# A two-layer hybrid trunk: the first layer's opening rebuilt, the filter network moved to the last scan

## The chip, the cores and the metric

One core of one Trainium2 chip runs the whole program. The metric is the device time of one execution in microseconds; each time of a kernel is the median of several executions. The profile is of one further execution. TensorE (PE) has two clock levels, 1.2 and 2.4 GHz; the profile gives the granted clock as a share of the upper one.

## The reference

Two layers work on 640 tokens of width 1024: 512 latent tokens and 128 context tokens, each group with its own conditioning vector. Per layer:

```python
shift, scale, gate = split(silu(cond) @ w_mod + b_mod, 3)      # cond (1024), w_mod (1024, 3072)
h = rmsnorm(x, g_pre) * (1 + scale) + shift
proj = h @ w_in                       # 8208 columns: four mixers of 2048, and 16 for A's decay and beta
ya = gated_delta_rule(conv3(q, k, v), decay, beta) * silu(z)   # A, 4 heads, scan over chunks, two directions
yb = hyena(...)   # B, long filters from a small network: sin(sin(feat @ w1 + b1) @ w2 + b2) @ w3 + b3
yc, yd = neighbourhood_attention(...), differential_attention(...)
y = sum_k sigmoid(h @ w_merge_k + b_k) * (y_k @ w_branch_k) @ w_out
x = x + gate * rmsnorm(y, g_post)
```

Everything is float32 outside and inside. Large products are made of three: weights and activations are split into a high part and a rest (`hi`, `lo`), and hi·hi, hi·lo and lo·hi are added.

## The kernel before

The engines run programs of their own, in an order written out by hand; they meet in semaphores, each wrapped in a `Signal` with a starting value. The functions named below follow in the listing.

**Start.** SP raises 120 semaphores to their starting values (L366), then `started`, for which every engine waits (L355) before its first load or its first work. SP then loads x, six pairs of modulation blocks, the first block of `w_in`, two more pairs, and the further weight blocks. POOL's queue loads nine constants (L447, all engines wait for all nine), then the filter network's weights and features, `lam`, the gate columns and the level masks (L458 to L468).

**Modulation, first layer.** w_mod's blocks for the 1024 shift and the 1024 scale channels go in pairs: pair p is the p-th block of 128 shift channels and the p-th of 128 scale channels. `mod_products` (PE) multiplies the conditioning (two columns padded to 32) with both blocks, 32 matmuls, into rows spread over four groups of 32 partitions. `rows_out` (ACT) copies them to `mod_rows`. `mod_channels` (PE) turns rows to channels and adds the four groups by a matmul with `pick`, a 128 x 2 matrix of ones at the right places. DVE adds the bias and makes `g_scale`. The rows of w_mod come through four slots: `raw` 0-1, `raw` 2-3 and two in `merged`. Further sixteen pairs (post gate and layer 1) go one by one into the merges (`later_pair`, L328), three in each merge as long as there are any.

**Activations, first layer.** ACT sums the squares of five tiles (L1466), POOL takes the power -1/2 (L456), DVE scales (L2035). PE turns x by transposes, eight times five (`turn_input`), after pair 1; ACT copies each turned k to `xT`; with pair p's channels ACT makes `modulated(p-1)`, and DVE splits it (`h_split`). When all eight pairs are through, PE runs the eight pieces of the first block (`project(..., KT)`, 6 matmuls a piece), then the 16 gate columns in both halves (`ab_half`), then block 1 with small turns of the gates between its pieces.

**The filter network.** Per layer two products of 64 rows by 640 (`hidden`), each followed by an argument reduced to one turn on DVE (`argument`, six operations) and a sine on ACT. Layer 0 does it at the very start; layer 1's stands in layer 0's output stage. B is the first to use its result, late in A's merge.

**Head 0.** Behind the gate columns come softplus, exp and sums (DVE L2060 to L2080, ACT L1487 to L1495). PE waits for their last result, `ab_done`, then runs block 2. ACT splits blocks 2 and 3 (`split_hi`) and then takes block 0 from PSUM; DVE does its share (`split_lo`), then the convolutions. `A_front` turns the convolved tiles, and so on; 16 fronts a head. Then levels of the triangular solve and five scan steps (`A_scan`, `A_step`); with the last head, PE fills the scan's gaps with pieces of the merge's first block (`last_part`). After the scan DVE squares the outputs, POOL takes the power, DVE norms them, PE turns them for the merge.

**Layer 1** has no opening: its h comes tile by tile from layer 0's output stage. PE has half of the gate columns and half of blocks 0 and 1 done by then, and does the other halves: gate columns first, then block 0, small turns, block 1.

Of the kernel before, what the change touches and what calls it, by code (L numbers as in the profile page):

```python
# [44 lines left out]
def program(nc, I, O):  # L45
# [3 lines left out]
    with ctx:  # L49
# [38 lines left out]
        cond, pick = view(cond_t, KT, 32), sb("pick", [128, 2])  # L88
# [11 lines left out]
        hid_t = sb("hid", [65, NT])  # L100
        gate_sg_t = sb("gate_sg", [128, 2, NT])
# [47 lines left out]
        raw_in = [Signal(f"raw_in{s}", SPLIT_BLOCKS // RING, step=16) for s in range(MOD_RING)]  # L149
# [4 lines left out]
        mod_in, later_in = ([Signal(f"{n}{i}", 0, step=16) for i in range(2)] for n in ("mod_in", "later_in"))  # L154
        mod_mm, mod_row, mod_sel = (Signal(n, KT + MOD_PAIRS) for n in ("mod_mm", "mod_row", "mod_sel"))
        mod_pair_in = [mod_in[0], raw_in[2], mod_in[1], raw_in[3]]
        xt_out = Signal("xt_out", KT)
        pad_zero = Signal("pad_zero", 1)
        level_cast = Signal("level_cast", 0)
# [4 lines left out]
        cond_ready, cond_zero, pick_ready = (Signal(n, 0) for n in ("cond_ready", "cond_zero", "pick_ready"))  # L164
# [68 lines left out]
        feat = pre.take(NT)[0:HY_EMB]  # L233
        hy_w12 = pre.take(2 * HY_FF)[0:HY_FF]
        hid_tmp = pre.take(2, NT)[0:HY_FF]
# [80 lines left out]
        mod_slots = [raw[:, 0:2], raw[:, 2:4], view(merged_t, 2, KT, 128), view(merged_t, 2, KT, 128, at=2 * D)]  # L316
        mod_slots += [mod_slots[1], mod_slots[2], mod_slots[3], mod_slots[1]]
        mod_frees = [0, 0, 0, 0, 2, 3, 4, 5]
        xT = [view(area, KT, NT)[:, k, :] for k in range(KT)]

        def mod_rows_at(c, x):

            return M[:, 512 * c + x:512 * c + x + 128]
# [26 lines left out]
        AB_AT, GC_AT, MOD_CH = 1664, 1792, 1024 + HALF + 128  # L350
# [3 lines left out]

        def start(eng):  # L355

            eng.wait_ge(started, 1)
# [5 lines left out]
        def _(sp):  # L363
            for s in Signal.all:
                if s.per and s.first:
                    sp.sem_inc(s.sem, s.first)  # L366
            sp.drain().then_inc(started, 1)
            start(sp)

# [5 lines left out]
            for layer in range(DEPTH):  # L375
# [3 lines left out]
                def load_pair(p):  # L379

                    into = mod_pair_in[p % 4]
                    if mod_frees[p]:
                        sp.wait_ge(mod_mm.sem, mod_mm.at(0, mod_frees[p]))
                        held(sp)
# [16 lines left out]
                if layer == 0:  # L401
                    for p in range(6):
                        load_pair(p)
# [279 lines left out]
        def _(pe):  # L683
# [39 lines left out]
            for layer in range(DEPTH):  # L723
# [660 lines left out]
                if layer == 0:  # L1384
                    pe.wait_ge(hid_arg.sem, hid_arg.at(1, 2))
# [1384 lines left out]
```

## Time and profile before

| | |
|---|---|
| median of 3 runs (lowest to highest) | 2917.41 us (2915.4 to 2917.65) |
| profiled execution: time, span | 2913.63 us, 2912.0 us |
| mean granted clock | 0.982 |
| loads and stores | 188.83 MB, mean 65 GB/s |

Times in rows are from the span's start. "PE" are matmuls, "PEld" their weight loads, SP and POOL with a q behind are their DMA queues. A row of the timeline merges like instructions that follow each other; its number after the start is the time in which they kept the engine busy. In brackets stand the idle time before it and what ended it. PE's instructions overlap, so the next starts before the busy time of one is over.

### The profile page before, as it was taken

The page shows a single profiled execution, that of the slowest core. Times are in us where ns is not written, and L with a number is a line of the kernel's source. Part 1 is how long each engine was busy: PE and PEld are TensorE (multiplying, and loading weights), DVE is VectorE, ACT ScalarE, POOL GpSimd, SP SyncE. Part 2 cuts the span into 40 slices and gives each one's busy share as a digit, 9 for nine tenths or more (in the row PEclk, how much of TensorE's full clock was granted, in tenths as well). Part 3 has the DMA queues.
Part 4 walks back from the last instruction along what each step waited for, and adds up shares of the span by engine and source line. Part 5 has one row for each costly group of instructions (what it writes and reads, how often), then busy time and mean ns, then how long its engine had stood idle before and what let it go on. Part 6 is the DMA issues. An engine that isn't in the chain of part 4 may idle for free. (4 is left out here: it accounts for less than half of the span.)

```text
span 2912.0 us, 49922 instructions
## 1 busy us (share of the span) xinstructions
PE 2715.1 (93%) x20104; PEld 2563.8 (88%) x20104; DVE 1479.9 (51%) x2366; ACT 973.7 (33%) x1675; POOL 371.0 (13%) x365
## 2 busy tenths in 40 slices
PE   3898999999999999998998999899999999999998
PEld 2798889999998889888987898899999988998798
DVE  3457655357733433554555567642776333345534
ACT  3423332232323432443254333322332244234422
POOL 1213312100000000110014124310000000011100
PEclk9899999999999999999998999999999999999999
DMA  5100100311132123222221000013111212222132
GB/s 197 62 23 19 33 17 12 122 67 43 46 102 89 61 71 98 77 71 102 94 87 39 20 29 26 19 49 115 41 52 60 75 60 70 66 82 61 55 103 80
DMA packets 53263, 188.83 MB, mean 65 GB/s; under 512 B 8152, under 2 KB 8318, under 8 KB 52928
## 3 DMA queue, kind: packets, MB, share of 16 engines
q1 hardware_dynamic: 40304, 147.34, 15.6%
q0 software_dynamic: 12752, 38.59, 4.2%
q8 instruction: 147, 2.41, 0.4%
q14 instruction: 60, 0.49, 0.1%
HBM read 173.31 MB, written 8.39 MB: 62 GB/s over the span
## 5 line engine op out<-in xcount | busy, mean ns | idle before, releaser
L689 PE MATMUL proj<-h_hi,w_hi 128*128 128x320 f32 x3072 | 746.7, 324 | 12.6 <-DVE w_lo L1930 10.1
L689 PE MATMUL mix<-area 128*128 128x128 f32 (+7 forms) x5056 | 686.4, 298 | 57.4 <-DMA area<-in_feat 27.9
L689 PE MATMUL proj<-h_lo,w_hi 128*128 128x320 f32 x3072 | 706.8, 311 | 0.0
L689 PEld LDWEIGHTS mix<-area 128*128 128x128 f32 (+4 forms) x5056 | 582.8, 187 | 138.9 <-issue 101.8
L689 PE MATMUL proj<-h_hi,w_lo 128*128 128x320 f32 x3072 | 702.3, 311 | 0.0
L1930 DVE TENSOR_TENSOR w_lo<-raw,w_hi 128x1024 fp32r<-128x1024 f32 x232 | 299.7, 1293 | 546.0 <-ACT w_hi L1424 546.0
L689 PEld LDWEIGHTS proj<-h_hi,w_hi 128*128 128x128 f32 x3072 | 510.7, 191 | 27.8 <-issue 19.6
L689 PEld LDWEIGHTS proj<-h_lo,w_hi 128*128 128x128 f32 x3072 | 520.2, 190 | 0.0
L689 PEld LDWEIGHTS proj<-h_hi,w_lo 128*128 128x128 f32 x3072 | 517.3, 189 | 0.0
L1424 ACT ACTIVATE area<-mix 128x512 f32<-128x512 f32 (+6 forms) x470 | 227.1, 512 | 761.1 <-PE mix L689 571.1
L1424 ACT ACTIVATE w_hi<-raw 128x1024 fp32r<-128x1024 f32 x232 | 245.3, 1058 | 687.1 <-PE proj L689 491.7
L2146 DVE COPY_PREDICATED area<-level,mix 128x512 f32<-128x512 uint8 (+1 forms) x288 | 163.8, 631 | 162.2 <-PE mix L689 162.1
L692 PE MATMUL mix<-ident,area 128*128 128x128 f32 x872 | 136.8, 290 | 82.4 <-ACT area L1424 36.7
L692 PEld LDWEIGHTS mix<-ident,area 128*128 128x128 f32 x872 | 105.6, 148 | 102.5 <-issue 63.7
L1930 DVE TENSOR_TENSOR area<-area 128x512 f32<-128x512 f32 (+6 forms) x234 | 159.3, 712 | 34.1 <-ACT merged L1853 13.2
L456 POOL TENSOR_TENSOR stat<-stat,neg_half 128x5 f32<-128x5 f32 (+2 forms) x40 | 50.2, 1256 | 860.5 <-DVE stat L2115 414.7
L689 PE MATMUL mix<-y_hi,w_hi 128*128 128x320 f32 x512 | 121.5, 319 | 0.2
L689 PE MATMUL mix<-y_lo,w_hi 128*128 128x320 f32 x512 | 117.2, 310 | 0.0
L689 PE MATMUL mix<-y_hi,w_lo 128*128 128x320 f32 x512 | 117.0, 310 | 0.0
L1424 ACT ACTIVATE area<-proj 128x640 f32<-128x640 f32 (+4 forms) x208 | 82.9, 452 | 87.8 <-PE proj L689 67.9
L689 PEld LDWEIGHTS mix<-y_hi,w_hi 128*128 128x128 f32 x512 | 85.0, 190 | 4.6 <-issue 3.2
L1790 ACT ACTIVATE area<-mix,stat 128x640 f32<-128x640 f32 (+1 forms) x80 | 56.0, 705 | 93.0 <-DVE stat L2479 92.9
(280 smaller groups left out, 2749.2 us busy)
## 6 DMA issues: line engine op xcount, KB each, us to landing
raw<-in_w_in SPq DMA_DIRECT2D x128, 512.0 KB, 3.6
raw<-in_w_mb SPq DMA_DIRECT2D x96, 512.0 KB, 3.6
raw<-in_w_mod POOLq DMA_DIRECT2D x32, 512.0 KB, 4.7
raw<-in_w_out SPq DMA_DIRECT2D x16, 512.0 KB, 3.6
out_x<-area SPq DMA_DIRECT2D x10, 512.0 KB, 2.6
area<-in_x_sample SPq DMA_DIRECT2D x2, 2048.0 KB, 9.0
raw<-in_w_mod SPq DMA_DIRECT2D x8, 512.0 KB, 8.8
merged<-in_w_mod SPq DMA_DIRECT2D x8, 512.0 KB, 10.4
```

What stands on the lines that cost most here:

```text
L456: P.tensor_tensor(stat[:, at:at + cols], stat[:, at:at + cols], neg_half[:, 0:cols], ALU.pow).then_inc(done_sig.sem, done_sig.step)
L689: return T.matmul(out, l, r, start=start, stop=stop)
L692: return T.transpose(out, src, ident[:, :])
L1424: return A.activation(out, x, ACT.Copy, scale=scale)
L1790: last = A.activation(D_p[:, i % 2, j, cols], D_scores[j][:, cols], ACT.Exp, bias=stat[:, 2 * m + j:2 * m + j + 1], accum_out=stat[:, 16 + ...
L1930: return V.tensor_tensor(out, a_, b_, op)
L2146: last = V.copy_predicated(out, mask, data)
```

## The change

- **Start.** Loads go out before the wait for `started`. SP loads x, pairs 0 and 1, block 0 of w_in, pair 2, and only then waits. PE, ACT and DVE raise a third of the semaphores each. POOL loads the constants first and then waits. Pairs have three slots of their own (`raw` 2-3, two in `merged`); `raw` 0-1 are for w_in alone.
- **Modulation.** `mod_channels` is two transposes, and DVE adds the four groups with a reduction (`mod_sums`), in the opening and for the sixteen later pairs. `pick` is gone.
- **Opening.** PE's order is written out: products, channels, turned x and pieces of the first block of different pairs take turns. Turned x goes from PSUM straight into `modulated`, without the copy to `xT`. The level masks are loaded by POOL after six pairs' products, and cast on DVE after the first convolution.
- **Filter network.** In both layers: `hidden` in steps 0 and 3 of the last head's scan, the argument in two parts on DVE (`argument`, `argument_rest`), the sines on ACT after step 2 and after the split of block 19. It writes to M's first 640 columns. Features, weights and scratch have moved to `hid`, `gate_sg` and a buffer of their own.
- **Head 0, both layers.** ACT takes block 0 and splits 2 ahead of the gate arithmetic, DVE convolves and splits likewise; PE no longer waits for `ab_done`. In layer 1 PE does block 0's half ahead of the gate columns' half.

```diff
+        def begin(eng, i):
+            for s in Signal.all[i::3]:
+                if s.per and s.first:
+                    eng.sem_inc(s.sem, s.first)
+            eng.drain().then_inc(started, 1)
+            start(eng)
         def start(eng):
-            eng.wait_ge(started, 1)
+            eng.wait_ge(started, 3)
...
+                if layer == 0:                       # SP
+                    load_pair(0)
+                    load_pair(1)
+                    load(0, I["w_in"][0, 0, 0, :, :])
+                    load_pair(2)
+                    start(sp)
+                    for p in range(3, KT):
+                        load_pair(p)
...
                 if layer:                            # POOL
                     pool.wait_ge(x_back.sem, x_back.at(layer - 1, TILES))
                 else:
-                    pool.wait_ge(level_cast.sem, 1)
+                    pool.wait_ge(x_n.sem, x_n.at(0, 1))
                 held(pool)
                 P.memset(pad, 0.0).then_inc(pad_zero.sem, pad_zero.step)
+                if layer == 0:
+                    pool.wait_ge(mod_mm.sem, mod_mm.at(0, 6))
+                    held(pool)
+                    pool.dma_start(level_in[:, :], I["level"]).then_inc(level_here.sem, 16)
...
-                def mod_channels(at):                # PE
+                def mod_channels(outs):
                     for x in range(2):
-                        last = mm(M[:, at + 2 * x:at + 2 * x + 2], mod_rows[:, x, :], pick[:, :])
+                        last = tr(outs[x], mod_rows[:, x, :])
...
+                    rows(0)
+                    rows(1)
+                    channels(0)
+                    rows(2)
+                    channels(1)
+                    turned(0)
+                    turned(1)
+                    rows(3)
+                    channels(2)
+                    turned(2)
+                    rows(4)
+                    channels(3)
+                    turned(3)
+                    piece(0)
+                    rows(5)
+                    channels(4)
+                    turned(4)
+                    piece(1)
+                    rows(6)
+                    channels(5)
+                    turned(5)
+                    piece(2)
+                    piece(3)
+                    rows(7)
+                    channels(6)
+                    turned(6)
+                    piece(4)
+                    channels(7)
+                    turned(7)
+                    piece(5)
+                    piece(6)
+                    piece(7)
...
+                    half_block(0, 1).then_inc(block_done.sem, block_done.step)     # layer 1
                     ab_half(1, 1).then_inc(ab_mm.sem, ab_mm.step)
-                    half_block(0, 1).then_inc(block_done.sem, block_done.step)
...
-                pe.wait_ge(ab_done.sem, ab_done.at(layer, 1))
...
                         def between():               # A_scan's gap
+                            if h == HEADS - 1 and n == 0:
+                                hidden(0, 0)
+                            if h == HEADS - 1 and n == 3:
+                                pe.wait_ge(hid_sin.sem, hid_sin.at(layer, 1))
+                                hidden(1, 0)
...
+                    rows(0)                          # ACT
+                    rows(1)
+                    split_hi(0, 0, 0)
+                    rows(2)
+                    turned(0)
+                    turned(1)
+                    for p in range(3, KT):
+                        rows(p)
+                        turned(p - 1)
+                    turned(KT - 1)
...
                 A_take(0, 0)
+                A_hi(2)
+                if layer == 0:
+                    lam_exp(0)
                 # the gates' exp and ln
                 A_take(0, 1)
                 # the decays' exp
+                A_hi(3)
                 A_silu(0, 0, 2)
...
+                def mod_sums(out, rows, bias):       # DVE
+                    V.tensor_reduce(out, rows.rearrange("p x (s r) -> p x s r", s=4)[:, :, :, 0:2].rearrange("p x s g -> p x g s"), AX.X, ALU.add)
+                    fence()
+                    return add(out, out, over(bias.unsqueeze(2), 2, 2))
...
+                    shift_and_scale(0)
                     dve.wait_ge(x_rn.sem, x_rn.at(layer, 1))
                     # the five normalisations
+                    shift_and_scale(1)
+                    split_lo(0, 0, 0)
+                    shift_and_scale(2)
+                    h_split(0)
+                    for k in range(3, KT):
+                        shift_and_scale(k)
+                        h_split(k - 2)
...
+                A_convolve(0, 0)
+                if layer == 0:
+                    dve.wait_ge(level_here.sem, 16)
+                    V.tensor_copy(level_t[:, :], level_in)
+                A_lo(2)
                 # the gates, as before, up to ab_done; A_convolve(0, 1) ahead of its last wait
+                A_lo(3)
...
                         A_step(h, n)                 # scan steps
                         if not more:
+                            if n in (0, 3):
+                                argument(int(n == 3))
+                            elif n == 1:
+                                argument_rest()
                             continue
...
                 A_out_squares(HEADS - 1)
+                argument_rest()
                 A_out_normed(HEADS - 1)
```

## Rows read from the trace of the kernel before

**Rows 1.** The page, busy time, share of the span, instructions
```profile
PE 2715.1 (93%) x20104; PEld 2563.8 (88%) x20104; DVE 1479.9 (51%) x2366; ACT 973.7 (33%) x1675; POOL 371.0 (13%) x365
```

**Rows 2.** Timeline and SP's line, opening: start, us, engine line op out<-in, idle and releaser
```profile
L366 SPq EVENT_SEMAPHORE  x120: 17/17/17, 1.0 to 8.4; - x120
...
20.02 1.28 ACT L1421 ACT_TABLE_LOAD   x1 [20.02 <-DMA small<-in_small]
...
27.92 2.36 PE L689 MATMUL mix<-area 33*64 33x512 f32 x4 [27.92 <-DMA area<-in_feat]
...
36.39 1.04 ACT L1466 ACTIVATE area<-area 128x1024 f32<-128x1024 f32 x1
...
41.10 1.21 POOL L456 TENSOR_TENSOR stat<-stat,neg_half 128x5 f32<-128x5 f32 x1 [17.51 <-issue]
...
45.01 3.39 DVE L2035 TENSOR_SCALAR area<-area,stat 128x1024 f32<-128x1024 f32 x5
...
45.34 1.94 PE L689 MATMUL mix<-raw,cond 128*32 128x128 f32 x32 [7.39 <-DVE area L2019]
```

**Rows 3.** SP's loads into raw before 30 us, issue to landing
```profile
L386 SPq DMA_DIRECT2D raw<-in_w_mod x4: 327/528/572, 9.8 to 11.4; - x4
...
DMA to landing us min/median/max: 11.6/12.9/13.9
```

**Rows 4.** Single operations: line L692 in 53:54.3 and 57.6:59, the rest timeline
```profile
L692 PE MATMUL proj<-ident,area x8: 421/421/421, 52.7 to 54.2; 128*128 128x128 f32 x8
...
L692 PE MATMUL proj<-ident,area x12: 272/273/421, 57.2 to 59.0; 128*128 128x128 f32 x12
...
59.69 1.08 PE L689 MATMUL mix<-merged,cond 128*32 128x128 f32 x32
...
62.38 0.82 DVE L1930 TENSOR_TENSOR h_lo<-gate_sg,h_hi 128x640 fp32r<-128x640 f32 x1
...
79.72 0.73 PE L689 MATMUL proj<-h_hi,w_lo 128*128 128x320 f32 x2
...
82.25 0.46 PE L689 MATMUL proj<-h_hi,w_lo 128*128 128x320 f32 x2
```

**Rows 5.** One stretch: PE, PEld, DVE, ACT, POOL busy, PEclk, DMA, GB/s
```profile
70.00:74.00 4.00, 3.25 (x44) 2.29 (x36) 1.92 (x5) 1.64 (x4) 0.00 (x0) 0.50 0.74 286
```

**Rows 6.** Timeline after the first block, layer 0
```profile
86.66 0.46 PE L689 MATMUL proj<-h_hi,w_lo 128*128 128x320 f32 x2
...
106.14 0.80 ACT L1424 ACTIVATE area<-proj 128x320 f32<-128x320 f32 x3
...
108.27 0.87 PE L689 MATMUL proj<-h_hi,w_hi 128*128 128x320 f32 x2 [5.06 <-DVE w_lo L1930]
...
110.83 0.89 DVE L2093 SCALAR_TENSOR_TENSOR area<-area,small 128x641 f32<-128x641 f32 x1
...
117.94 1.06 PE L692 MATMUL mix<-ident,area 128*128 128x128 f32 x8 [0.65 <-ACT area L1531]
```

**Rows 7.** Timeline of PE at the start of layer 1
```profile
1516.85 0.32 PE L689 MATMUL mix<-h_hi,ab_w_hi 128*16 128x320 f32 x1
...
1534.94 0.87 PE L689 MATMUL proj<-h_hi,w_hi 128*128 128x320 f32 x2 [5.06 <-DVE w_lo L1930]
```

**Rows 8.** Timeline of DVE and PE in layer 0's output stage
```profile
1441.43 1.22 DVE L1930 TENSOR_TENSOR y_lo<-raw,y_hi 128x1024 fp32r<-128x1024 f32 x1
...
1441.58 1.29 PE L689 MATMUL mix<-area 33*64 33x512 f32 x4
```

**Rows 9.** Layer 0's last scan: a stretch (columns of Rows 5), then timeline
```profile
495.00:502.00 7.00, 7.00 (x58) 7.00 (x57) 1.61 (x6) 0.77 (x2) 0.00 (x0) 1.00 0.01 2
...
502.20 0.61 DVE L2159 SCALAR_TENSOR_TENSOR area<-area,ab_s,mix 128x128 f32<-128x128 f32 x2 [3.19 <-PE mix L689]
...
521.46 0.82 DVE L1930 TENSOR_TENSOR merged<-merged,stat 128x640 f32<-128x640 f32 x1 [1.42 <-POOL stat L456]
...
522.35 1.33 PE L692 MATMUL mix<-ident,merged 128*128 128x128 f32 x5 [4.46 <-DVE merged L1930]
```

**Rows 10.** Timeline of PE in a merge, a later modulation pair
```profile
550.08 0.50 PE L689 MATMUL mix<-pick,mod_rows 128*128 128x2 f32 x4
```

More of the change, by code:

```diff
@@ L363, in _ @@
         def _(sp):
[L364 to L368, printed above, removed]
             def load_x():
@@ L401, in _ @@
                 if layer == 0:
-                    for p in range(6):
-                        load_pair(p)
-                    load(0, I["w_in"][0, 0, 0, :, :])
-                    load_pair(6)
-                    load_pair(7)
                     for u in range(1, HEADS * UNIT):
@@ L797, in _, with channels @@
-                    piece = project(layer, 0, 0, 0, 0, KT)
-                    for k in range(KT):
-                        pe.wait_ge(h_ready.sem, h_ready.at(0, k + 1))
-                        piece(k)
+                        out = mod_rows_at(p)
+                        mod_products(mod_slots[p % 3], [out[:, 0, x, :] for x in range(2)])
+                    def channels(p):
+                        pe.wait_ge(mod_row.sem, mod_row.at(0, p + 1))
+                        out = mod_rows_at(p)
+                        mod_channels([out[:, 1, x, :] for x in range(2)])
@@ L1621, in _ @@
                         if not more and n == 2:
+                            sine(layer, 0)
                             act.wait_ge(block_done.sem, block_done.at(layer, base(0) + 17))
@@ L1627, in _ @@
                 A_hi(19)
+                sine(layer, 1)
+                A.drain()
                 def merge(b):
@@ L1879, in _ @@
                     out_hi(n, block_done, base(4))
-                if layer == 0:
-                    sine(1, 0)
                 for n in (4, 5):
@@ L1887, in _ @@
                     y_first(t)
-                    if t == 2 and layer == 0:
-                        sine(1, 1)
                 for n in (6, 7):
@@ L1919, in _ @@
             V.memset(cond_t[:, :], 0.0)
-            start(dve)
+            begin(dve, 2)
             held(dve)
@@ L2587, in _ @@
                 out_lo(2)
-                if layer == 0:
-                    argument(1, 0, 1024)
                 out_lo(3)
@@ L2604, in _ @@
                     V.tensor_scalar(stat[:, Y_FIRST + t:Y_FIRST + t + 1], stat[:, Y_FIRST + t:Y_FIRST + t + 1], 1.0 / D, EPS, ALU.mult, ALU.add)
-                    if t == 1 and layer == 0:
-                        argument(1, 1, 1024)
                 out_lo(6)
```

260 lines of the change are left out of this document (107 added, 153 removed).

## The prediction

> **What bounds the kernel now.** I read the page first: PE is busy 93% of the span [rows 1], so time is only to be had where PE waits, runs at its low clock, or does work that isn't needed. The tenths of the span put the one large hole in the first slice and a half. So I read the timeline of the first 90 us, then the stretches with the granted clock, then the waits of PE at the four other places that the change touches: the start of head 0 in both layers, the last scan, the output stage, a merge.
>
> The opening is a chain of waits. SP raises 120 semaphores from 1.0 to 8.4 us before any engine or load starts; the constants are there at 20.02; PE first works at 27.92, when POOL's feature load has landed, and that is the filter network; its two sine arguments sit on DVE ahead of the normalised x, which is done at 45.01+3.39 = 48.4; the modulation products start at 45.34, behind the second argument (7.39 us of wait) [rows 2]. Then comes pair after pair, each a ping-pong of PE, ACT and DVE, with the granted clock at 0.50 (the 1.2 GHz level) though PE is busy 3.25 of 4 us [rows 5]. The first block runs only after the last pair, and ends at 86.66+0.46 = 87.1 [rows 6].
>
> **The opening, step by step.** The waits on `started` no longer stand ahead of the loads, so both load queues start some 7.5 us earlier (the semaphores took 1.0 to 8.4). POOL's constants then land near 20.0-7.6 = 12.4. ACT's table load of 1.28 and the SiLU take it to 14.0. SP's queue holds x, then pairs 0 and 1. Before, the loads of the first two pairs were issued from 9.8 to 11.4 and took 11.6 to 13.9 us [rows 3], so they landed from 21.4 to 25.3; 7.6 earlier gives 15 for pair 0 and 17.7 for pair 1. x is ahead of them in the queue.
> - ACT: five squares of 1.04 from 14.0 to 19.2; POOL's power 1.21 [rows 2], so 1/rms at 20.7.
> - PE: products of pair 0 at 15.3, of pair 1 at 17.7, each 1.94 at the low clock [rows 2]; their rows are copied when ACT is through the squares, turned at 19.7, summed on DVE (about 0.8) by 21.1.
> - DVE: five normalisations, 3.39 [rows 2]: x is normalised at about 24.6, against 48.4. So 23.8 us come from here.
> From there PE's own work sets the pace. A turn of one k is 5 transposes that start 0.21 apart at the low clock (8 of them from 52.7 to 54.2) and about 0.13 at the full one [rows 4]. A pair's products are 1.94 or 1.08 [rows 2, 4], of which the next instruction waits 1.6 or 0.85. A pair's channels are now 2 transposes, 0.42 or 0.26. A piece of the first block is 6 matmuls, 0.73 for two or 0.46 for two with overlap [rows 4], 1.6 or 0.88 a piece. Left after 24.6: 8 turns, 5 products, 6 channels, 8 pieces. That is 8.6+8.0+2.5+12.9 = 32.0 at the low clock, 5.2+4.3+1.6+7.0 = 18.1 at the full one. Neither list is free of waits: the first piece needs turn, ACT, then DVE's split (0.82 and its cast, [rows 4]), and so does the last; following the written order engine by engine, I get 3 us of waits at the low clock, 7 at the full one. End of the first block: 59.5 all low, 49.5 all full. I take 55, the clock rising around 40, when pieces of 128 x 320 are in the mix. Against 87.1 that is **32.0** (27.5 to 37.5).
>
> What the row shows of the clock: the transposes went from 421 to 273 ns in the stretch from 51.8 to 59, in which PE did nothing else than transposes [rows 4], that is, the clock rose under them; and products alone, with PE 81% busy, did not raise it [rows 5]. The Trainium skill (TensorE: Matmul & The Clock Gate, Part 4: PE-mode transpose) says that transposes don't count as work for the clock, which speaks against a chain rebuilt out of them. The trace here disagrees by 421 against 273. By that rule the opening would stay low, and the sum would be that of the second case below.
>
> **After the first block, layer 0.** Before: PE had 108.27-5.06-87.1 = 16.1 us of work (gates' columns, block 1, small turns), then waited 5.06 for DVE's w_lo, because ACT and DVE split blocks 2 and 3 only behind the gate arithmetic, and PE itself waited for `ab_done`; block 2 then ran at the low clock until 117.94-0.65 = 117.3, 9.0 us [rows 6]. After: the copy of block 0 (0.80), its convolution (three operations of at most 0.89, [rows 6]), the level cast and split 2 lie under those 16 us. Block 2 follows at once, at full clock: 24 pairs that start 0.29 apart, 7.0. 16.1+7.0 against 30.8 is **7.5** saved. The level load moves on POOL's queue behind pair 5; POOL's power and pad are ahead of it, and DVE wants it only after the first block, so nothing waits. Bounds: 5.0 (the wait alone, if block 2 stays slow) to 8.2. What is late next: the first transposed tiles of head 0, whose copies stand behind the third convolution on ACT; this wait stays.
>
> **Layer 1's start** repeats it: a wait of 5.06 and a slow block [rows 7]. But here PE has only half a gate product, 24 matmuls in 3.5 us (it starts near [rows 7]'s first line), between block 0's half and the small turns. The row that these need stands on DVE behind copy, convolution and split: 0.8+2.6+1.2, then its own 0.8, and hops: 5.8. New wait 2.3. So 5.06+2.0+0.6-2.3 = **5.3**, taken as **5.0** (3 to 6.5).
>
> **The filter network.** Layer 0's share of the opening is counted above. In the output stage of layer 0 two sets of 1.29 leave PE, but the first lay under DVE's y_lo, which ends at 1442.65 against 1442.87 [rows 8]: it saves 0.2, the second 1.0 or so, **1.2** (0 to 2.4). In the last scan of each layer PE is busy 7.00 of 7.00 [rows 9]: nothing covers the two sets, 1.1 each before the next matmul starts. DVE idles 3.19 in a scan step [rows 9], so the first half of an argument (about 2) and its rest (2.2) fit between steps, and ACT's sine with its table load fits before the next copy. The last rest doesn't: it stands between the squares and the normed output, where DVE waited 1.42 for POOL and PE 4.46 for DVE [rows 9]; three operations of 640 columns take 2.3, so +0.9 (0 to 1.3). Per layer 2.2+1.0 = 3.2, **6.4** lost in both (4.4 to 8).
>
> **Later pairs.** Sixteen times four matmul records of the pick (0.50, [rows 10]; the next work starts 0.36 later) become two transposes, 0.26: **1.0** saved, taken low. DVE gets a reduction and a fence, 0.3, in merges where PE sets the pace; bound: -3 if that is on the path each time.
>
> **Sum** against the profiled execution, 2913.6: 32.0+7.5+5.0+1.2+1.0-6.4 = 40.3, so 2873.3. The median of the runs shown, 2917.41, is 3.8 above it, so the forecast is **2877.1** (its own range 2869 to 2885).
>
> **Rivals.**
> - The opening keeps the low clock until the first block ends (59.5): 4.5 less, 2881.6. For: [rows 5], low at 81% busy. Against: the transposes raised it [rows 4]. Chance 0.2.
> - The full clock comes with the first turns: 51 or so, 2873. Chance 0.08.
> - Loads at once gain less. SP now puts 6 MB ahead, and the constants share the engines with it; if they are served behind x and the first pairs (before, these took until 25.3, so until 17.7), the products start 4 to 5 us later: 2882. For: that queue is full from the first microsecond. Against: the constants were sharing with these loads before, too, and took 20.0 while the pairs took 25. Chance 0.12. The Trainium skill (DMA: Bandwidth & Descriptors, Queues, rings and completion order) has the engines take turns between queues by packet, by which the constants would not be served last; the order in [rows 2, 3] agrees.
> - The waits at head 0 only move: PE waits on the fused gate and weight steps instead, both starts give the wait back (12.5 us): 2889. For: layer 1 already shows a new wait of 2.3. Against: 16 us of cover in layer 0. Chance 0.12.
> - The moved loads or waits do not take effect, because an engine still holds the others up (PE, ACT and DVE each raise a third of the semaphores before they work): no change within 0.2%, chance 0.02.
> - Slower: a clock that falls in the opening's interleaving and does not come back in head 0. At 0.50 PE's work takes nearly twice as long, so each us of PE work is priced at nearly one more. To eat 40 us it must hold for some 80 us beyond the first block. For: the stretch at 0.50 though 81% busy [rows 5]. Against: dense blocks bring it back each time, the second piece pair of [rows 4] within 3 us. At 90 us of it: 2922. Chance 0.03.
> The forecast has the rest, 0.43.
>
> **The numbers.** 0.2%, 6 us, is about what a measurement can tell from no change. Faster: all but the last two, 0.95; same 0.02; slower 0.03. The range takes the cases from the early clock, 2866 with its bounds, to lost gains at head 0 with the filter at its dearest, 2892.
>
> **What would show it.** The normalised x near 25 and first pieces near 34; the first block's end near 55, with the clock to be read there; no wait of 5.06 before block 2 in either layer, and one of 2 to 3 before layer 1's small turns; scans longer by 2.2 and a wait of 5.4 in place of 4.46 behind each; transposes of 2 per pair in the merges. I am wrong if the first block ends after 65, if PE waits inside a last scan, or if the constants land after 16.

## The result and the profile after

The changed kernel takes 2871.34 us (median of four runs, 2870.0 to 2873.47), the kernel before beside it 2916.51 (2915.4 to 2917.65): a ratio of 0.9846, 95% interval 0.9829 to 0.9863. The forecast was 2877.1 (2866 to 2892). The profiled execution has a span of 2868.5 us against 2912.0, so 43.5 are to be explained.

The page's busy line, which answers to [rows 1]: PE works 17.5 us less and is otherwise as full as before. The other 26 of the 43.5 us are time in which it no longer stands still.

```profile
PE 2697.6 (94%) x20056; PEld 2547.6 (89%) x20056; DVE 1480.1 (52%) x2389; ACT 967.7 (34%) x1666; POOL 374.8 (13%) x365
```

The timeline of the opening after, against [rows 2, 4]. Nine constants are there at 13.20 (20.02 before), x is normalised at 25.97 (48.4; five operations from 22.57, 3.40 in all), the first turns of x follow at once, and the third pair's products already take 1.08:

```profile
1.00 0.44 SPq L368 DMA_DIRECT2D area<-in_x_sample  x1
...
13.20 1.28 ACT L1452 ACT_TABLE_LOAD   x1 [13.20 <-DMA small<-in_small]
...
16.72 1.94 PE L690 MATMUL mix<-raw,cond 128*32 128x128 f32 x32 [16.72 <-DMA raw<-in_w_mod]
19.19 1.93 PE L690 MATMUL mix<-merged,cond 128*32 128x128 f32 x32 [0.53 <-DMA merged<-in_w_mod]
...
23.04 1.08 PE L690 MATMUL mix<-merged,cond 128*32 128x128 f32 x32 [1.54 <-DMA merged<-in_w_mod]
...
26.02 0.76 PE L693 MATMUL mix<-ident,area 128*128 128x128 f32 x5 [1.54 <-DVE area L2086]
...
46.88 0.56 PE L690 MATMUL proj<-h_hi,w_hi 128*128 128x320 f32 x2 [1.56 <-DVE h_lo L1961]
...
50.83 0.74 PE L690 MATMUL proj<-h_hi,w_lo 128*128 128x320 f32 x2
51.37 0.47 PE L690 MATMUL mix<-h_hi,ab_w_hi 128*16 128x320 f32 x1
```

The first block ends at 50.83+0.74 = 51.6, not at 87.1 [rows 6]. The stretches (PE, PEld, DVE, ACT, POOL busy, granted clock, DMA share, GB/s) show what sets the pace towards its end: from 40 to 48 the clock is high, and PE is busy only 2.44 of 4 us, because its pieces wait for DVE's `h_lo` (0.69, 1.56 and 1.56 from 38 to 47). The last two pieces run in the row of 0.57.

```profile
20.00:24.00 4.00, 2.46 (x58) 1.64 (x50) 2.02 (x7) 1.50 (x3) 1.21 (x1) 1.00 1.03 409
...
40.00:44.00 4.00, 2.44 (x43) 2.00 (x38) 1.79 (x5) 0.91 (x2) 1.06 (x2) 1.00 0.68 246
44.00:48.00 4.00, 2.44 (x17) 1.95 (x15) 2.89 (x7) 1.66 (x5) 0.00 (x0) 1.00 0.50 199
48.00:52.00 4.00, 3.84 (x16) 3.46 (x16) 2.55 (x4) 1.35 (x4) 0.00 (x0) 0.57 0.11 8
```

PE's timeline at the starts of head 0, against [rows 6, 7]. Block 2 follows the gates' sums at once; the wait for ACT's copies at the fronts stays (3.82, where it was 3.33), and the second layer has its new wait of 2.04:

```profile
67.37 0.39 PE L690 MATMUL mix<-ab_s,ones 128*128 128x40 f32 x2
67.59 0.54 PE L690 MATMUL proj<-h_hi,w_hi 128*128 128x320 f32 x2
...
79.57 0.69 PE L693 MATMUL mix<-ident,area 128*128 128x128 f32 x2 [3.82 <-ACT area L1455]
...
1482.62 0.61 PE L690 MATMUL mix<-ident,tmp 16*128 16x16 f32 x4 [2.04 <-DVE tmp L2218]
```

The end of layer 0's last scan and a later pair, against [rows 9, 10]:

```profile
468.12 1.29 PE L690 MATMUL mix<-gate_sg,hy_w 64*64 64x512 f32 x4
...
471.13 0.54 PE L690 MATMUL proj<-h_hi,w_hi 128*128 128x320 f32 x2
...
482.42 1.33 PE L693 MATMUL mix<-ident,merged 128*128 128x128 f32 x5 [5.33 <-DVE merged L1961]
...
510.20 0.38 PE L693 MATMUL mix<-ident,mod_rows 128*128 128x128 f32 x2
510.33 0.54 PE L690 MATMUL mix<-y_hi,w_hi 128*128 128x320 f32 x2
```

**The ledger.** For each instruction that stands in both kernels, its start after minus its start before gives how far ahead the changed kernel is; the differences between two places are what lies between them. The first mark is the gate row copy: DVE copies the gate columns' products out of PSUM (the line with `ab_row`). It is the last instruction of the opening that all the kernels have.

| stretch | gained, us | forecast |
|---|---|---|
| opening, to the gate row copy (94.35 to 58.93) | 35.4 | 32.0 |
| head 0, layer 0, to its first exponentials (126.98 to 84.01) | 7.5 | 7.5 |
| levels of heads 0 to 3, layer 0 | 1.0 | - |
| last scan, layer 0 (-43.98 to -39.88) | -4.1 | -3.2 |
| merges: sixteen pairs of 0.22 to 0.23 | 3.6 | 1.0 |
| merges of layer 0: one spell more at the low clock | -1.3 | - |
| output stage, layer 0 | 2.4 | 1.2 |
| start of layer 1 | 5.5 | 5.0 |
| last scan, layer 1 (-48.08 to -43.30) | -4.8 | -3.2 |
| the rest | -1.7 | - |
| sum, to the end of the span | 43.5 | 40.3 |

The start of layer 1 is taken up to PE's wait at the fronts. Up to the first exponentials, the mark of layer 0, it is 4.4. Of the last row's -1.7, 1.0 is given back between PE's wait at the fronts of layer 1 and its last scan (-49.03 to -48.08).

### The profile page after: what moved, and what is told of

The parts are those of the page before. It is cut to its first block and busy times, and to the rows that moved or that the text cites. A ratio compares the mean times of both kernels' runs of the same rounds, so it can differ in the third digit from the quotient of the medians.

```text
span 2868.5 us, 49890 instructions
## 1 busy us (share of the span) xinstructions
PE 2697.6 (94%) x20056; PEld 2547.6 (89%) x20056; DVE 1480.1 (52%) x2389; ACT 967.7 (34%) x1666; POOL 374.8 (13%) x365
## 5 line engine op out<-in xcount | busy, mean ns | idle before, releaser
L690 PE MATMUL mix<-area 128*128 128x128 f32 (+7 forms) x5040 | 679.7, 298 | 24.6 <-DVE area L2159 15.6
L1455 ACT ACTIVATE area<-proj 128x320 f32<-128x320 f32 (+4 forms) x200 | 77.7, 442 | 86.3 <-PE proj L690 71.6
```

The source lines that it names most:

```text
L690: return T.matmul(out, l, r, start=start, stop=stop)
L1455: return A.activation(out, x, ACT.Copy, scale=scale)
```

## The experiments

Each is compared with the kernel before on the same chip. By that the changed kernel stands at -45.2 us (2871.34 against 2916.51), and at -42.4 when run again, so differences of 3 us between medians are not read; smaller ones are read from the traces. "Clock loss" is the sum over stretches of 4 us, up to 2860 us, of 4 x (1 - granted clock), in us: what PE loses if it has work all the time. Before it was 53.0, after 42.6 (53.4 and 44.7 over the whole spans). It leaves out the slow work before the clock first rises, for there the rows read 1.00: the kernel before has its first pairs' products at 1.94 until 51 in such rows, the changed one until 21.

**The same kernel again.**

> The changed kernel as it is, profiled a second time. Theory: the granted clock follows from what TensorE did, so TensorE's high clock stands again from about 22 us on (the third modulation product starts at 23.0 in the first profile and takes 1.08 us where the first two took 1.94 and 1.93), and the first block ends within 2 us of 51.5; span within 3 us of 2868.5. Rival: the early high clock was the luck of one execution; then the third product or several more take 1.9 us and the first block ends at 54 to 57, and the span is 3 to 6 longer.

2872.12 against 2914.47, span 2867.9. The theory held for the span. Of the opening it held half: the third product took 1.25, the fourth 1.94 again, and the granted clock stood at 0.50 and 0.65 from 24 to 32, where the first profile had 1.00:

```profile
24.00:28.00 4.00, 3.19 (x24) 2.29 (x14) 3.43 (x7) 1.13 (x3) 0.64 (x1) 0.50 1.02 405
28.00:32.00 4.00, 3.72 (x54) 2.84 (x56) 0.97 (x5) 1.82 (x5) 0.00 (x0) 0.65 0.57 200
```

Yet the first block ended only 1.2 us later, at 52.7 (the gate row copy 1.03 later), since this run had no dip at 48 to 52. Its clock loss is 42.6 too.

The first profile was a lucky one at this place. Ten more profiles (this one and nine of those below) have the same work on PE up to the third pair. Its product took 1.08 in one of them, `e_old_start`, and 1.25 to 1.94 in the nine others. In the six profiles whose opening is the changed kernel's unaltered (this one, the first, and `e_ab_done`, `e_no_filter`, `e_pick_later`, `e_fronts`) the gate row copy starts between 58.49 and 60.97. So 33.4 to 35.9 is what the opening gives, and a difference of 2 us at that mark between single profiles can be the clock's.

**The start.** Two runs, one that takes the new start away from the changed kernel, one that gives it alone to the kernel before.

```diff
 # e_old_start, in the changed kernel
+for s in Signal.all: sp.sem_inc(s.sem, s.first)     # SP, all 120, before its first load
+sp.drain().then_inc(started, 1)
 # e_start_alone, in the kernel before
-for s in Signal.all: sp.sem_inc(s.sem, s.first)
+for s in Signal.all[i::3]: eng.sem_inc(s.sem, s.first)   # PE, ACT and DVE, a third each
+load_pair(0..3) ahead of SP's wait, POOL's constants ahead of its own
+P.memset(neg_half); held(pool); P.drain()     # POOL, ahead of its nine constants instead of behind
```

> The changed kernel with only the old start: SyncE raises all 120 semaphores itself before any load, and the loads of raw weights, constants and x are issued behind that. Theory: the loads' order of issue makes the whole opening late by what they are late: the raises occupied SyncE from 1.0 to 8.4 us before, so the constants land 6 to 7.5 us later and x is normalised as much later; the end +6 to +8 us (2877.5 to 2879.5 by median), with everything between the normalised x and the first block's end of the same length. Rival: what bounds the opening is the chain of DVE and TensorE behind the modulation weights' products, and the later loads are half hidden: +2 to +4.

> The kernel before with only the new start: semaphores raised by three engines in thirds, the raw weights of the first four pairs loaded at once, gpsimd's loads before its wait for the raises; the modulation, the order of the first block and all the rest as before. Theory: the opening is a chain from the landing of the constants, so it moves as a whole by 6 to 8 us: 2908.5 to 2910.5 by median. Rival: the chain before was bound by its 16 hidden steps and the low clock and not by the landing, or the clock falls differently, and less than 3 us of it is kept (above 2913.5).

The first: 2882.01, -32.5 us in place of the -42.4 that the changed kernel had on that chip. The gate row copy is 7.29 late, head 0 of layer 0 7.3 late too: the opening moves as one block by what the raises took. (The other 3 us of its span of 2879.3 lie in the merges and at the start of layer 1, with 46.1 of clock loss.) The second: 2903.6 against 2914.47, so -10.9, more than expected. In its trace the features had landed at 14.69 where they took until 27.92 [rows 2], 13.2 earlier instead of 7:

```profile
14.69 2.36 PE L695 MATMUL mix<-area 33*64 33x512 f32 x4 [14.69 <-DMA area<-in_feat]
...
32.57 1.72 PE L695 MATMUL mix<-raw,cond 128*32 128x128 f32 x28 [7.40 <-DVE area L2025]
```

The other 6 us are not the raises'. The kernel before has no wait for the constants at this place, but a `P.drain()` stands between the nine constant loads and the feature load, and POOL idled 6.95 us there. The new start puts it ahead of the nine, and so does `e_old_start`, which has the old raises: it issues the same loads 6.6 us earlier. First the kernel before, then `e_old_start`:

```profile
13.80 0.14 POOL L448 MEMSET neg_half<- 128x16 f32 x1
20.89 0.53 POOL L459 DMA_DIRECT2D area<-in_w  x1 [6.95 <-issue]
```

```profile
13.73 0.54 POOL L451 DMA_DIRECT2D small<-in_small  x1
14.26 0.55 POOL L461 DMA_DIRECT2D hy_w<-in_w  x1
```

The start is worth 7.3 where the opening doesn't need the features, and 11.5 at the gate row copy where it does and the drain is moved too; the wait of 7.40 before the products stays what it was.

**The filter network out of the opening.**

```diff
-hidden(0, 0); hidden(1, 0)      # PE, with the waits for their sines
-argument(0, 0, 0); argument(0, 1, 0)    # DVE
-sine(0, 0); sine(0, 1)          # ACT
+A.activation(hid_t[0:HY_FF, :], x_tm[0:HY_FF, 0, 0:NT], ACT.Copy)
```

> The kernel before with the filter network left out of its opening (its two products, arguments and sines of the first layer; the filter's input gets a copy of x instead). Everything else, the raises ahead of the loads too, is as before. Theory: the network is half of the opening's gain by itself: x's squares no longer stand behind its first sine (34.71) and the modulation's first product no longer behind its second argument (a wait of 7.39 to 45.34), so the first product starts 20 to 24 us earlier and the normalised x is done 13 to 16 us earlier; the gate row copy and the end come 14 to 20 us earlier: 2896 to 2902 by median. With the start alone at 11 us and no overlap between the two this leaves 5 to 10 of the opening's 35 for the transposes and the order. Rival: the time would go into the clock or a later wait, and the gain is under 8 us.

2898.15 against 2914.98, -16.8; the gate row copy 16.3 earlier, x's power 11.7. Its first product starts at 22.74, 22.6 before [rows 2]'s 45.34, but the pairs then run at the low clock again, with their hops of 0.50 (the second line's stretch has a granted clock of 0.50):

```profile
47.39 1.93 PE L689 MATMUL mix<-raw,cond 128*32 128x128 f32 x32
49.83 1.01 PE L689 MATMUL mix<-pick,mod_rows 128*128 128x2 f32 x4 [0.50 <-ACT mod_rows L1417]
```

How the opening's 35.4 divide can be read from a chain of four kernels, each with one group of changes more than the one above it (the order of the loads and POOL's drain come with the third), by their gate row copies:

| kernel | network in the opening | turning, order, loads | semaphore raises | gate row copy, us | step |
|---|---|---|---|---|---|
| before | yes | old | old | 94.35 | |
| e_open_no_filter | no | old | old | 78.09 | 16.3 |
| e_old_start | no | new | old | 66.22 | 11.9 |
| changed | no | new | new | 58.93 | 7.3 |

So the network is 16.3, the transposes, the interleaving and what else changed in the opening 11.9, the start 7.3. Adding the start of 11.5 and the network of 16.3 would leave 7.7 for the rest, as the expectation above has it, but very likely counts the late features twice, since they are the network's input: the start alone gained 11.5 with the network behind it and 7.3 without. Each step is a difference of single profiles, good to 1 or 2 us. The 11.9 were not divided further: turning by transposes, PE's order and the direct path into `modulated` were never tried apart.

**Pieces last.**

```diff
-piece(k) between the pairs
+piece(0) ... piece(7) behind the last pair's turn of x
```

> The changed kernel with the first block's pieces all behind the last modulation pair, as in the kernel before, in place of between the pairs. The eight pieces take 0.46 us each at the high clock and 0.73 at the low one. Theory: TensorE has holes between 36 and 48 us (busy 2.4 of each 4 us), so interleaving fills holes: with the pieces last the opening ends 3 to 4 us later (six pieces by 0.46 plus what DVE's last h_lo leaves); the end +3 to +4. Rival A: pieces are also what keeps the granted clock high in the holes; with them gone the clock falls and the end is +6 to +9. Rival B: DVE's chain bounds it and the last pieces wait for DVE in either order: under +1.5.

2870.21 against 2914.47, -44.3: no loss. The gate row copy came 2.18 earlier. From the 40-us mark PE runs the pieces without a hole, each two matmuls in 0.46, and has done at 49.35 although the products still took 1.94 and 1.72 until 30 here:

```profile
42.24 0.54 PE L690 MATMUL proj<-h_hi,w_hi 128*128 128x320 f32 x2
...
49.06 0.46 PE L690 MATMUL proj<-h_hi,w_lo 128*128 128x320 f32 x2
49.35 0.31 PE L690 MATMUL mix<-h_hi,ab_w_hi 128*16 128x320 f32 x1
```

(The expectation calls 0.46 and 0.73 the time of a piece; they are the time of two of its six matmuls.) The theory falls, and rival B isn't quite it either: the pieces didn't fill holes, they made them. A piece between pairs stops PE until DVE has split that k (0.69, then 1.56 twice), and the products behind it, on which DVE's next step depends, are late by that. The medians don't separate the two orders (-44.3 and -42.4), but in the traces the new place is clear: of the profiles in which the fourth product was still slow, those with the pieces between have the gate row copy at 59.96 to 60.97, the two with the pieces last at 56.75 and 56.42.

**Head 0's order, and one wait of it.**

```diff
 # e_ab_done: this line alone, ahead of block 2
+pe.wait_ge(ab_done.sem, ab_done.at(layer, 1))
 # e_head0_old: that line, and ACT, DVE and PE in the old order behind the first block
```

> The changed kernel with head 0's work after the first block put back into the old order in both layers: the products behind ab_done, ab_half before half_block, ACT's exponential first and its takes late, DVE's A_lo(2) and convolutions late. Theory: this order is worth what it moved at the fronts, 7.4 us in the first layer and 5.5 in the second; the end comes 12 to 13 us later (2883 to 2885 by median). Rival: the waits would only have moved on, and the old order costs less than 8 us in all, since part of it is hidden behind TensorE's blocks.

> The changed kernel with only one wait back: TensorE waits for DVE's rows of a and b (ab_done) before the second block's products, in both layers. Theory: TensorE enters the second block at 67.6 now and DVE ends ab_done near 71.1, so block 2 begins 3.5 us later in the first layer, and about 3 us later in the second; 5 to 7 us in all if everything behind it is bound by TensorE's blocks. Rival: ACT's and DVE's fronts end the wait before the fronts anyway (PE waits 3.82 there), and that wait swallows it: under 2 us in all.

2884.08 against 2916.41, -32.3, for the whole order: 10 to 13 us lost (12 to 13 expected). But the one wait loses as much, 2885.01, -31.4, which is 11 to 14 in place of the 5 to 7 expected; a surprise. Its trace has the wait twice, 7.2 in all, as expected, and 52.9 of clock loss in place of 42.6. Waits of PE and stretches in this kernel, with the second of the two waits at 1505.88:

```profile
PE proj L690 <- DVE ab_s L1963: 7.2, 2, 3.7
...
1496.00:1512.00 16.00, 12.56 (x55) 12.47 (x55) 5.18 (x15) 8.10 (x15) 3.22 (x1) 0.63 0.11 34
...
1492.00:1496.00 4.00, 2.23 (x11) 2.19 (x12) 1.91 (x6) 0.00 (x0) 0.00 (x0) 0.78 0.42 131
1496.00:1500.00 4.00, 4.00 (x16) 4.00 (x16) 1.10 (x7) 1.99 (x5) 0.00 (x0) 0.50 0.00 0
...
1504.00:1508.00 4.00, 2.12 (x8) 2.15 (x9) 2.71 (x4) 3.90 (x7) 2.24 (x1) 0.56 0.07 12
1508.00:1512.00 4.00, 4.00 (x19) 4.00 (x18) 0.00 (x0) 0.12 (x1) 0.99 (x1) 0.59 0.36 123
...
1505.88 0.87 PE L690 MATMUL proj<-h_hi,w_hi 128*128 128x320 f32 x2 [3.44 <-DVE ab_s L1963]
```

The changed kernel at the same work, and `e_pick_later`, which has no such wait, behind its own gate row copy at 1483.74:

```profile
1486.00:1502.00 16.00, 12.15 (x80) 11.65 (x80) 7.62 (x16) 11.26 (x21) 3.14 (x1) 0.91 0.10 34
```

```profile
1484.00:1488.00 4.00, 3.39 (x15) 3.36 (x16) 1.19 (x6) 0.54 (x4) 0.00 (x0) 0.62 0.40 131
1488.00:1492.00 4.00, 4.00 (x17) 4.00 (x17) 0.75 (x4) 1.45 (x2) 0.00 (x0) 0.53 0.01 4
```

In the 16 us PE is as busy as in the changed kernel (12.56 and 12.15) for 55 matmul records against 80. 7.2 of waiting and 10.3 of clock are 17.5 of the span's 19.3. But not all of the 10.3 belongs to the wait. The stretch holds two low spells, and the first (0.78 and 0.50 from 1492) was over before PE began to wait at 1502.4; `e_pick_later` has the same one without the wait. Behind the second wait 3.4 us are lost (0.56 and 0.59), behind the first, which ends at 73.54, 1.7 (rows of 0.79 and 0.79 from 72 to 80, where the changed kernel's rows are 1.00 up to 76). That makes 7.2 + 5.1 = 12.3, which fits the 11 to 14 by medians; the profiled execution was the slowest of the four, and the rest of its clock loss lies elsewhere. That these two spells follow from the waits is argued from their place and not shown by a run of its own.

Old order and single wait end up level, though the old order has 1.3 us more of waiting: its clock loss is 51.3. Its profile too is that of the slowest of four executions.

**The filter network in the last scan.**

```diff
-hidden(0, 0), hidden(1, 0), argument, argument_rest and sine in the scan
+A.activation(hid_t[0:HY_FF, :], h_lo_v[0:HY_FF, 0, :].bitcast(f32), ACT.Copy)
```

> The changed kernel without the filter network in the last scan (its two products, arguments and sines are left out, and the filter's input for the second half gets a copy instead). Theory: in both layers the scan is TensorE, DVE and ACT in turn, and the network costs what the two traces showed, 4.3 and 4.8 us, so 9 us less in all, 2862 to 2864 by median, and the wait before the output's product falls from 5.33 to 4.46. The prediction had 6.4 for it. Rival: DVE's and ACT's steps of the network lie in waits that are there anyway, and only the two products of 1.29 count: 5 us.

2868.97 against 2916.41, -47.4: 2 to 5 us gained, not 9. Compared step by step with the changed kernel, the scan itself shortens by 1.41 behind the first product, 1.41 behind the second, 0.88 at the end, where the wait is 4.46 again: 3.70 in layer 0, and 3.71 in layer 1.

```profile
480.73 1.12 PE L693 MATMUL mix<-ident,merged 128*128 128x128 f32 x4 [4.46 <-DVE merged L1952]
```

So the network costs 7.4 in both layers, not 6.4 and not the ledger's 8.9. The other 1.5 of the ledger are not shown to be its doing. This trace gave 2 us back in its opening and 3 in layer 1's heads (44.4 of clock loss).

**The old turning in the merges.**

```diff
-mod_channels([mod_rows_later[:, x, :] for x in range(2)])     # two transposes
+last = mm(M[:, 1472 + 2 * x:1474 + 2 * x], mod_rows[:, x, :], pick[:, :])   # x in 0, 1
```

> The changed kernel with the later modulation pairs (16 in the merges) turned by the old product with a selecting matrix and added by DVE, in place of two transposes and a sum that DVE reads over. Theory: 0.22 to 0.23 us for each of the 16 pairs as the sigmoids in the merges showed, 3.6 in all, +3 to +4. Rival: as the prediction had it, only TensorE's own 0.06 to 0.12 a pair counts, +1.

2875.79 against 2916.41, -40.6. The sigmoids behind each pair fall back by 0.23 a pair (-0.47, -0.24, -0.01, then 0.23, 0.45, 0.68, and so on), which times sixteen is 3.6. The ledger's loss of 1.3 in layer 0's merges is one spell more at the low clock: from 1180 to 1330 the changed kernel has three (below), the kernel before two (1228 and 1320), and this kernel also two (1232 and 1280). So it is most likely the clock's and not the change's, though both profiles of the changed kernel have all three:

```profile
1184.00:1188.00 4.00, 3.29 (x15) 3.32 (x16) 1.94 (x4) 0.56 (x2) 0.00 (x0) 0.63 0.01 4
1232.00:1236.00 4.00, 3.98 (x19) 3.96 (x20) 2.73 (x7) 0.00 (x0) 0.00 (x0) 0.60 0.02 4
1296.00:1300.00 4.00, 2.60 (x12) 2.63 (x13) 1.55 (x4) 2.12 (x5) 0.00 (x0) 0.71 0.28 103
```

**Reorderings of the changed kernel.** The waits that are left point at four: DVE's split ahead of the next scale from step 6 on (only in `e_best`; `e_best2` has the pieces last instead), `argument_rest` behind the normalisation, ACT's first copies and DVE's row copy first.

```diff
 # fronts, both layers and all three kernels
+A_front(0, 0); A_front(0, 1)      # ACT, ahead of these two
 A_hi(4)
 A_silu(0, 2, 1)
 # layer 1, all three: the row copy ahead of A_lo(2) on DVE
 # e_best, e_best2
 A_out_squares(HEADS - 1)
-argument_rest()
 A_out_normed(HEADS - 1)
+argument_rest()
```

> The changed kernel with four small reorderings: DVE's split of h ahead of the next scale from step 6 on, the last part of the second argument behind the scan's normalisation, and in both layers head 0's first copies on ACT and, in the second layer, the row copy on DVE ahead of loads' splits. Theory: 0.9 a layer at the scan's end (the wait for the output goes from 5.33 back to 4.46), 2 to 3 in the opening, 1 to 2 at the second layer's start; 5 to 7 us less, 2864 to 2867 by median. Rival: each wait is shared by another engine's chain that ends just behind it, or what is gained comes back as time at the low clock (one spell of it costs 3.4 us); under 2 us in all.

> The changed kernel with the first block's pieces all behind the last modulation pair (the gate row copy came 2.2 us earlier in such an order) and the three reorderings that don't concern the opening: the second argument's last part behind the scan's normalisation, head 0's first copies on ACT first, and the second layer's row copy first on DVE. Theory: 1.3 to 2.2 for the pieces, 1.8 for the argument, 1 to 2 for the second layer's start: 4 to 6 us less, 2865 to 2868 by median. Rival: the clock takes it back, 2870 to 2873.

> The changed kernel with head 0's first two front copies moved ahead on ACT (ahead of a weight split and one silu) in both layers, and in the second layer the row copy ahead of a weight split on DVE; nothing of the opening or the scan's end. Theory, from the two traces with all the reorderings: TensorE's wait of 3.82 for ACT's copies at head 0's fronts falls to about 0.5 in each layer, and the wait before the second layer's small turns from 2.04 to 1.1; 3.3 + 3.3 + 1.0 = 7.6 us less, 2863 to 2865 by median, the rest of the 15.5 of the joint kernels being opening, scan and clock. Rival: the 15.5 came mostly from the opening and from fewer spells at the low clock, and the fronts give under 4 us (above 2867).

| kernel | median, us | before, us | ratio, 95% interval | clock loss |
|---|---|---|---|---|
| e_fronts | 2860.11 | 2913.56 | 0.9817, 0.9801 to 0.9834 | 40.2 |
| e_best | 2855.79 | 2914.98 | 0.9798, 0.9782 to 0.9815 | 39.0 |
| e_best2 | 2855.05 | 2914.98 | 0.9797, 0.9781 to 0.9813 | 35.7 |

Both full versions beat both kernels, by 59 to 60 us against before, 14 to 18 ahead of the changed kernel, over twice what was expected; between the two of them 0.8 us decides nothing. The fronts alone gave 8 to 11, because the 3.82 of wait falls to 0.54, and then head 0 is at once on: in e_fronts the gate row copy is 1.22 late against the changed kernel, head 0's first scan step 1.85 early and its normalisation 2.30; in layer 1 the lead grows from 3.87 at the row copy to 9.52 at the first scan.

```profile
77.51 0.44 PE L693 MATMUL mix<-ident,area 128*128 128x128 f32 x2 [0.54 <-ACT area L1455]
```

PE's waits for ACT's copies, all of them, changed kernel and then e_fronts: 6.9 less.

```profile
PE mix L693 <- ACT area L1455: 37.4, 30, 3.8
```

```profile
PE mix L693 <- ACT area L1455: 30.5, 29, 3.0
```

In e_best the opening gives 4.0 (the split first), in e_best2 2.5 (the pieces last); both have the 4.46 wait back in both scans, 0.9 each. Clock loss is 3.6 and 6.9 less than in the changed kernel. The parts of the openings are of the size of the scatter of 58.49 to 60.97, and which of the reorderings took the spells away was not tried.

## Why the prediction was right, point by point

- **The sum, 40.3 forecast, 43.5 in the span.** Every term has the right sign. By the ledger they were short by 3.4 in the opening, 2.6 in the later pairs, 1.2 in the output stage and 0.5 in layer 1, and the network was charged 2.5 too little (1.0 by the run that leaves it out); 2.0 net went where nothing was forecast. That the sum is nearer than its terms is in part luck: the opening and the later pairs gave more, the network and the rest took more.
- **The normalised x**: 24.6 said, 25.97 measured. DVE makes pair 0's scale ahead of the normalisation, and its channels stand on PE behind pair 1's products; these started at 19.19 instead of 17.7, and that is the whole delay. The constants at 13.2 instead of 12.4 (POOL's queue starts 7.1 us earlier, not 7.6) didn't count, since 1/rms was there at 21.58 and the scaling began at 22.57. The rival in which the constants come after SP's 6 MB fell: they came before pair 0. The bound of 16 for them held.
- **From there to the first block's end**: 30.4 said, 25.6 measured. The step that failed was "the clock rising around 40, when pieces of 128 x 320 are in the mix". It had risen by 23, in the second run for good by 31, and in all eleven profiles of the rebuilt opening it was high when the first piece started. The ends were 51.6 and 52.7. That is the second rival's case (51 or so), which had a chance of 0.08; its 2873 is nearer to 2871.34 than the forecast's 2877.1. The "7 us of waits" at the high clock were right in kind and too many: the timeline has 4.3 behind the first turn, 0.69 + 1.56 + 1.56 of them for DVE's split.
- **Transposes and the clock.** In the first profile the turns of x ran at the high clock, five in 0.71, with nothing but transposes and pairs' products around them until 31, and the clock stayed at 1.00 through them. In the second profile the same chain ran at the low clock from 24 to 31 (five turns in 1.27), and then rose under it. So the chain doesn't always hold the high clock, but it did bring it back each time. The Trainium skill's rule (TensorE: Matmul & The Clock Gate, Part 4: PE-mode transpose), weighed in the prediction, would have given the low clock until the first block's end; the traces again disagree.
- **Head 0, layer 0**: 7.5 said, 7.5 measured, and the way as well: cover by the 16 us of PE's work, block 2 at the high clock from 67.59, and the wait at the fronts that stays. (The two sums written down, 30.8 and 23.1, differ by 7.7; the wait at the fronts grew by 0.5.) That the waits only move was the wrong rival; e_head0_old gives the 10 to 13 us of both layers back.
- **Layer 1's start**: 5.0 said with a new wait of 2.3; 5.5 (4.4 by layer 0's mark) and 2.04.
- **The network**: 6.4 said, 7.4 measured by leaving it out, 3.7 a layer. The mis-sized term is PE's two sets: 1.1 each taken, 1.41 each found, of which 1.29 are the matmuls themselves. The remainder, 0.9 of wait (4.46 to 5.33), was right to a tenth, and PE doesn't wait otherwise inside the scan.
- **Later pairs**: 1.0 said "taken low", 3.6 measured. The failed step is the 0.26 of two transposes, which counted both; the next matmul starts 0.13 after the first of them (510.20, 510.33) and stood 0.36 behind the pick. DVE's reduction and fence cost nothing on the path.
- **What the prediction lacked**: the price of low-clock spells. It counted 2.0 a block for them at head 0, but took the rest of the kernel as unchanged. The clock loss fell by 10.4. In the first 200 us, in the opening and head 0, it fell by 11.3, from 17.1 to 5.8; that is inside the terms above, and behind them the changed kernel loses 0.9 more than before.

```profile
0.00:200.00 200.00, 142.07 (x1081) 128.04 (x1082) 86.44 (x141) 67.88 (x127) 41.04 (x37) 0.91 0.28 100
```

```profile
0.00:200.00 200.00, 162.32 (x1358) 150.32 (x1359) 105.23 (x179) 76.39 (x144) 52.97 (x42) 0.97 0.29 103
```

The first is before, the second after. What stays open: what decides where a spell falls (the same kernel had one at 24 to 32 in one execution and at 48 to 52 in the other), how the 11.9 of the opening divide, and 0.7 of the ledger's last row.

## What to carry to other kernels

A wait of the busiest engine can cost more than its length: here 7.2 us of waiting cost 11 to 14 by medians, and low spells of 5.1 stand right behind the two waits. Whether a low spell belongs to a wait is only seen by looking for the same spell in a run without the wait. Before two changes are added up, run one with the other already in place: the start was worth 11.5 alone and 7.3 in company. Work put "in the holes" of an engine makes holes of its own if it depends on another engine's step, so place it behind the chain that sets the pace. And a first copy that others wait for goes ahead of weight splits on its engine: two such moves on ACT and one on DVE gave 8 to 11 us, beside the 35 of the whole rebuilt opening.

## What was unexpected of the hardware

- Behind waits of 3.74 and 3.44 before a dense block of 320-column matmuls the granted clock fell (rows of 0.79 and 0.79, and of 0.56 and 0.59), where the changed kernel without the waits has 1.00 at the first place. But a spell as deep stood ahead of the second wait too (0.78 and 0.50), and the same one in a kernel without the wait (0.62 and 0.53).
- The high clock came between 19 and 22 us, after two pairs' products of 1.94 and 1.93; in a second execution of the same program it fell back from 24 to about 31, and with the pieces last it came at 30. Over the eleven profiles of the new opening it rose for the chain of turns and pieces between 21 and 32, and the opening's end moved by only 2.5 us in the six with the same order.
- The granted clock doesn't show all slow work: the first two products took 1.94 and 1.93 in a stretch whose row says 1.00, where the third took 1.08. Single durations had to be read beside the column.
- With a `drain` behind nine load issues POOL idled 6.95 us, until 20.89, 0.9 after the constants were there; with it ahead of them the idle time was 0.66. A load issued behind it landed 13.2 us earlier when the drain was moved and 7 us of semaphore raises were taken away.
